# Triangular inverses turned on VectorE, a state-space stage without GpSimd, and three stages folded into their neighbours

## The reference, cut to what matters

```python
mod = silu(cond) @ w_ada + b_ada                     # shift, scale, gate, twice
h = rms_norm(x, norm1_g) * (1 + sc1) + sh1
z = h @ w_in                                         # r, k, v | wd, ad, gd (low rank) | u
y_r = rwkv7_mix(z[..., :OFF_U], state_rwkv, ...)     # 8 heads x 64, both directions
y_s = s5_mix(z[..., OFF_U:], state_ssm, ...)         # 32 groups x 16, one complex state of 64 per group
x = x + g1 * (concat(y_r, y_s) @ w_out)
h = rms_norm(x, norm2_g) * (1 + sc2) + sh2
x = x + g2 * (square(relu(h @ w_ff1)) @ w_ff2)
y = rms_norm(x, norm_f_g)
```

## Time and profile before

| what | value |
|---|---|
| median of 3 runs | 2572.7 us (2570.61 to 2576.2) |
| profiled execution, its own time | 2570.66 us |
| its span in the trace | 2568.7 us |
| front / stage u / state space | 0 to 105.2 / to 189.0 / to 472.5 us |
| GLU / low rank | to 573.3 / to 637.1 us |
| RWKV preparation / 36 steps / last step's rest and last finish | to 766.2 / to 1647.1 / to 1684.4 us |
| tail | to 2568.7 us |

### The profile page before, as it was taken

The page is one execution under the profiler, slowest core; times in us unless marked ns, Lnnn a source line. Parts: engine busy times, 40 slices in busy tenths (PEclk is TensorE's granted clock), DMA queues, the critical chain, the costliest instruction groups (busy, mean ns, idle before and its releaser), DMA issues. The chain is left out here.

```text
span 2568.7 us, 50592 instructions
## 1 busy us (share of the span) xinstructions
PE 2093.2 (81%) x21540; PEld 1373.1 (53%) x21540; DVE 1239.2 (48%) x2498; ACT 758.3 (30%) x1682; POOL 649.7 (25%) x720
## 2 busy tenths in 40 slices
PE   7673445475649899988898989769999999999998
PEld 2342334233436787677677778634555455455453
DVE  1469999730153545464546454434333333323325
ACT  2302223311123434343434444323322122112111
POOL 1407552212111212222222222113221211211253
PEclk9676777787769999999998999879999999999999
DMA  7200000441100000000000000052211011011112
GB/s 280 76 1 5 10 10 11 142 162 58 29 9 12 14 3 11 10 17 11 2 10 5 3 3 7 2 208 91 91 66 66 1 66 66 18 49 66 50 38 94
DMA packets 62691, 120.25 MB, mean 47 GB/s; under 512 B 5946, under 2 KB 25402, under 8 KB 61682
## 3 DMA queue, kind: packets, MB, share of 16 engines
q1 hardware_dynamic: 62468, 117.02, 12.9%
HBM read 97.56 MB, written 17.35 MB: 45 GB/s over the span
## 5 line engine op out<-in xcount | busy, mean ns | idle before, releaser
L83 PE MATMUL psum<-arena 128*128 128x384 bf16 (+3 forms) x2244 | 739.1, 335 | 125.1 <-ACT arena L1700 27.9
L84 PE MATMUL psum<-arena 128*128 128x384 bf16 (+3 forms) x2244 | 738.4, 335 | 0.0
L85 PE MATMUL psum<-arena 128*128 128x384 bf16 (+3 forms) x2244 | 737.6, 335 | 0.0
L1652 ACT ACTIVATE arena<-psum 128x256 f32<-128x256 f32 (+5 forms) x900 | 289.8, 333 | 529.1 <-PE psum L1524 141.4
L83 PEld LDWEIGHTS psum<-arena 128*128 128x128 bf16 (+1 forms) x2244 | 224.3, 100 | 311.5 <-issue 78.7
L85 PEld LDWEIGHTS psum<-arena 128*128 128x128 bf16 (+1 forms) x2244 | 224.9, 100 | 172.1 <-issue 9.7
L84 PEld LDWEIGHTS psum<-arena 128*128 128x128 bf16 (+1 forms) x2244 | 224.4, 100 | 164.1 <-issue 7.5
L2637 DVE TENSOR_TENSOR arena<-arena 128x384 f32<-128x384 f32 x96 | 106.9, 1113 | 234.7 <-ACT arena L2513 234.7
L1524 PE MATMUL psum<-arena 64*64 64x64 f32 x2880 | 179.7, 222 | 10.7 <-DVE arena L2201 10.7
L2652 DVE TENSOR_TENSOR arena<-arena,psum 128x512 f32<-128x512 f32 x108 | 74.2, 687 | 196.7 <-PE psum L85 196.7
L1524 PEld LDWEIGHTS psum<-arena 64*64 64x64 f32 x2880 | 159.4, 137 | 15.0 <-DVE arena L2201 14.8
(11 more groups left out here) (298 smaller groups left out, 3251.3 us busy)
## 6 DMA issues: line engine op xcount, KB each, us to landing
arena<-in_w_ff SPq DMA_DIRECT2D x16, 2048.0 KB, 8.5
arena<-in_w_ada SPq DMA_DIRECT2D x12, 2048.0 KB, 8.3
x<-arena SPq DMA_DIRECT2D x18, 512.0 KB, 2.8
arena<-x SPq DMA_DIRECT2D x18, 512.0 KB, 3.2
arena<-in_w_in SPq DMA_DIRECT2D x12, 512.0 KB, 4.0
arena<-in_x SPq DMA_DIRECT2D x9, 512.0 KB, 8.9
out_y<-arena SPq DMA_DIRECT2D x9, 512.0 KB, 2.7
arena<-in_w_out SPq DMA_DIRECT2D x2, 2048.0 KB, 10.6
```

The costliest lines, as they stand in the source:

```text
L83: nc.tensor.matmul(out, whi, xhi, start=first, stop=False)
L84: nc.tensor.matmul(out, wlo, xhi, start=False, stop=False)
L85: return nc.tensor.matmul(out, whi, xlo, start=False, stop=last)
L1652: copy = lambda out, src: nc.scalar.activation(out, src, ACT.Copy)
```

## The change

1. *Front.* Normalised blocks have nine buffers, so ACT and POOL do all nine norms ahead of the modulations; only L249 and L254 stay behind them. `w_ada` pieces 2 and 3 are queued on SP behind x blocks 0 to 5 and 0 to 7; the weights of u use the buffer of a `w_ada` piece and come last.
2. *State space.* POOL's 17-tap products go. DVE makes `gout` itself by another `complex_product` (`out_weights`), and PE makes the taps from `gout` and C. ACT loses its `gout` copies. In stage u three tap tables become two exit tables and a negated C. ys goes to memory in four parts during the GLU.
3. *Low rank.* The block goes; PE's 216 matmuls stand in the first preparation of `stage_rwkv` (`lora`, at `TO_LORA`).
4. *Inverses.* Only X is made by matmuls on levels below the last (L1523's kind), only the transpose on the last; DVE turns the copy (`flip`), and `begin` is DVE's too.
5. *Last finish* and *tail.* Two of three groups of the last finish lie among the last steps (`LAST_*` tables), and w_out and ys are loaded before the tail.

```diff
 # stage_front, SP
-            load(1)
-            load(2)
-            for b in range(TILES):
+            for b in range(NB):
                 keep_x(b)
-            weights(2)
-            weights(3)
+                if b + TILES < NB:
+                    load(b + TILES)
+                if b in (2, 4):
+                    weights(b // 2 + 1)
...
 # stage_front, ACT
-            for b in range(TILES, NB + TILES):
-                if b < NB:
-                    norm(b)
-                high(b - TILES)
+            for b in range(NB):
+                high(b)
...
 # stage_s5, ACT
                     weights(i + 1)
-                out_weights(i)
-                if more:
                     taps(i + 1)
...
 # stage_s5, PE tap
+                pe.wait_ge(ev("gout"), i + 1)
+                need(pe, ev("taps"), 2 * i)
+                        mm(ps[0:GC, TAP_FWD, g * P:g * P + GC], S.b[n][:, GB * i + g], c[:, GB * i + g], start=(n == 0), stop=(n == 1))
+                        last = mm(ps[0:GC, TAP_FWD, g * P + GC:(g + 1) * P], S.b[n][fwd, GB * i + g], flat[fwd, n, g, 0:AFTER],
...
+                        last = mm(ps[0:GC, TAP_BWD, g * AFTER:(g + 1) * AFTER], S.b[n][bwd, GB * i + g], flat[bwd, n, g, GC:],
...
 # stage_s5, DVE
+            def out_weights(i):
+                need(dve, ev("y"), 2 * (i - 1))
+                complex_product(nc.vector, dve, c, [gout[i % 2][:, 0], gout[i % 2][:, 1]], c4, p4, sc, neg_im=True, done=ev("gout"))
...
                     in_weights(i + 2)
                 if i + 1 < NBATCH:
+                    out_weights(i + 1)
                     rotor(i + 1)
                     skip(i + 1)
 # stage_rwkv, PE
+                        for n in H2:
+                            if pi < 0:
+                                yield z + TO_LORA[n]
+                                lora(n)
...
                             if l < NLEV - 1:
-                                mm(xblock(b, q, h, 0), xt, grow[b, l - 1, q, h], start=True, stop=True)
-                            last = mm(xblock(b, q, h, 1), grow[b, l - 1, q, h], xt, start=True, stop=True)
+                                last = mm(xblock(b, q, h, 0), xt, grow[b, l - 1, q, h], start=True, stop=True)
+                            else:
+                                last = mm(xblock(b, q, h, 1), grow[b, l - 1, q, h], xt, start=True, stop=True)
...
 # stage_rwkv, DVE
+            def begin(i):
+                for q in H2:
+                    dve.wait_ge(ev("xt0"), 4 * i + 2 * q + 2)
+                    nc.vector.transpose(xx[:, q, :, 0], xt0[:, q]).then_inc(ev("x0", q), 1)
+
+            def flip(i, l):
+                for q in H2:
+                    dve.wait_ge(ev("inv", l, q), i + 1)
+                    nc.vector.transpose(xx[:, q, :, 1], xx[:, q, :, 0]).then_inc(ev("flipped", l, q), 1)
+
             def merged(i, l):
+                if l > 1:
+                    flip(i, l - 1)
                 reset(i, l)
...
 # stage_rwkv, SP; stage_tail loses the same loads
+            for h in H2:
+                sp.dma_start(M.w_out[h], ins["w_out"][:, :, h * 512:(h + 1) * 512]).then_inc(ev("w_out"), 16)
+            sp.wait_ge(ev("x"), 6 * NCT)
+            for n, ys in enumerate((M.ys_hi, M.ys_lo)):
+                sp.dma_start(ys, ins["ys"][:, n]).then_inc(ev("ys"), 16)
```

More of the change, by code:

```diff
@@ L32 @@
 SEG = NC_ + 1
-TAPS = 2 * CH + 1
 GB = 4
@@ L170, in _ @@
             load(0)
+            load(1)
+            load(2)
             weights(0)
@@ L486, in s5_memory @@
     S.in_table = two(CH, G)
-    S.tap_table = [A.take(TAPS, G) for _ in range(3)]
+    S.out_table = two(CH, G)
     S.turn = two(SUP, G)
@@ L635, in stage_s5 @@
     sn = [A.take(2, GB, NC_) for _ in H2]
-    f = [A.take(2, GB, TAPS, GC) for _ in H2]
     gout = [A.take(2, GB, CH, GC) for _ in H2]
-    strip = [A.take(GB, TAPS - 2, GC, parts=GC) for _ in H2]
+    strip = [A.take(GB, 2 * CH - 1, GC, parts=GC) for _ in H2]
     toe = [A.take(GB, P) for _ in H2]
@@ L641, in stage_s5 @@
     tv = [A.take(GB * P) for _ in H2]
-    tg = [A.take(GB, TAPS, GC) for _ in H2]
     dd = A.take(G, GC, parts=GC)
@@ L1253, in stage_rwkv @@
     v = [A.take(NB, P) for _ in H2]
-    y = [A.take(NB, P), y1]
+    y = [A.take(NB, P) for _ in H2]
+    mt_at = A.at
     mt = [A.take(2, 2, 2, 64) for _ in range(6)]
@@ L1306, in periods @@
     def periods():
-        return [(pi, PERIOD * pi, pi + 1 if pi + 1 < NCT else None, pi - 1 if pi > 0 else None) for pi in range(-1, NCT + 1)]
+        return [(pi, PERIOD * pi, pi + 1 if pi + 1 < NCT else None, pi - 1 if pi > 0 else None) for pi in range(-1, NCT)]
     def entered_by(ct, d, g):
@@ L1378, in project, with lora @@
                 last.then_inc(ev("filled"), 1)
+            def lora(n):
+                pe.wait_ge(ev("lora_w_lo"), 1)
+                need(pe, ev("lora_f"), n)
+                for g in range(TG):
+                    for q in range(KD):
+                        last = split_mm(nc, ps[:, LORA.start + g, 0:GW], lw_hi[:, q, n], lw_lo[:, q, n], M.hi[:, q, cols(g)],
+                                        M.lo[:, q, cols(g)], q == 0, q == KD - 1)
+                last.then_inc(ev("lora"), 1)
             def sums(at, n):
@@ L1464, in beside @@
                         yield from entry(c, 1, 1, ENTRY[1, 1])
+                z, f = PERIOD * NCT, NCT - 1
+                for n in range(3):
+                    yield z + LAST_GATE[n]
+                    gate(z + LAST_GATE[n], f, GROUPS[n])
+                    yield z + LAST_TURN[n]
+                    turn_out(z + LAST_TURN[n], f, n, GROUPS[n])
             def score(u):
@@ L1917, in beside @@
                         split(3 * c + 2)
+                        if pi < 0:
+                            for n in range(3):
+                                yield z + TO_LORA[n]
+                                lora_low(n)
                         if c + 1 < NCT:
@@ L2713, in program @@
     keep_front = A.at
+    M.w_out = [A.t[:, M.hi_at + h * KD * 512:M.hi_at + (h + 1) * KD * 512].rearrange("p (k n) -> p k n", k=KD) for h in range(2)]
     s5_memory(M)
```

419 lines of the change are left out of this document (209 added, 210 removed).

## The result

The changed kernel takes 2531.0 us (median of 4 runs, 2529.7 to 2533.0) against 2571.7 for the kernel before; the ratio is 0.984, interval 0.983 to 0.985. That is 41 us less, where 96 had been forecast, and 1 us above the range.

The account below looks back on a forecast made before the run. Five stages had different limits, DVE in the state space, PE in the 36 steps. Terms -10 - 2.5 - 24 - 27 - 12 - 11.5 - 9 = -96 took 2570.66 to 2474.7, forecast 2475 us, range 2408 to 2530.

Parts of the forecast that it names:

- The state space: State space: first spin starts 19.5 us in, 26 earlier; seven batch intervals about even (+2.3); together -24 us.
- the taps' wait on ACT: State space: ACT's list has taps ahead of arrivals and waits for PE's tap, making a batch 31.3 us.
- Low rank and preparation: Low-rank block and first preparation: 63.8 us go, PE's 36.9 come back in the preparation; -27 us.
- The tail: Tail's start: ACT's 9.21 us wait for w_out goes, as the load moves among the last steps; -9 us.
- waits behind the flips: Steps, levels 4 and 5: PE waits about 0.7 us longer on each, 1.4 a bare step, leaving it 1.1 gain.
- the clock's term of the steps: 36 steps: PE's mean clock falls from 0.95 to 0.926, 21 us back against 33 gained, leaving -12.
- its sign of being right: Steps: a mean clock outside 0.91 to 0.96 would show the prediction wrong.
- the clock falling in the steps: Rival, steps: mean clock 0.90 costs PE 44 us more, kernel 2498; at 0.87, 73 more, 2527; chance 0.16.
- The lower bound of this term: Steps: -78 us if nothing is waited for, 89 less 11 for six steps and a little clock.
- the front: Front: w_ada queued behind 2.5 MB, 12 us at most, 9 taken, modulations start at 61; front 95 for 105.2, -10.
- 26.8 in a row: Front: POOL becomes the limit behind the modulations, 19.2 us of L249 and 7.6 of L254 without gaps.
- the last finish: Last finish: its second and third group leave the end, their 8.1 us of DVE work moving among bare steps; -11.5 us.

Follow-up runs that it names:

- run 6: The changed kernel with ScalarE's copies of the taps placed behind the arrivals and natural-order copies of a batch instead of ahead of them: 2492.8 us, ratio 0.970.
- run 3: The changed kernel without the eight flips of a step, TensorE reading X unturned, matmuls as few, the two transposes of begin kept: 2491.5 us, ratio 0.969.
- run 2: The changed kernel with the 64 merge matmuls a step put back as work nobody reads, the transposes on VectorE kept: 2560.5 us, ratio 0.996.
- Run 7: The changed kernel with the whole front stage of the kernel before (part 1 undone): 2526.8 us, ratio 0.983.
- run 1: The changed kernel with the inverses of the kernel before (part 4 undone), all else as changed: 2507.6 us, ratio 0.975.
- run 4: The changed kernel with the flips of levels 3 and 4 ahead of the two score masks on VectorE instead of behind them: 2501.3 us, ratio 0.973.
- run 9: The changed kernel with flips ahead of the score masks, ScalarE's taps behind the arrivals and the front of before: 2464.2 us, ratio 0.959.

## Why the prediction was wrong

*What held.* The state space: start (19.0 for 19.5), batch (31.8 for 31.3) and the reason, the taps' wait on ACT, which run 6 showed by moving it. Low rank and preparation -29.6 for -27. The tail -9.8 for -9. A flip 0.25 to 0.29 for 0.27. Two further agreements are luck. Step 33 came to 16.47 for 16.4, but the five steps 29 to 33 gained 0.8 together, not 1.1 each. TensorE's idle time rose by 41 us where 30 steps with 1.4 us, 42, were put in for waits behind the flips; but 26 of the 41 came with no flip at all (run 3), the flips add 15, and in step 33 the two waits rose by 0.8 only, from 0.15 and 0.28 to 0.55 and 0.67.

*What failed: the clock's term of the steps.* The step of the sum is "From a mean of 0.95 to 0.926: 797 x (0.95/0.926 - 1) = 21 back". The mean came to 0.85, outside the 0.91 to 0.96 that the prediction gave as its sign of being right, and the matmuls that remained were 69 us dearer. I had taken the fall from two rows, 1.00 in a bare step and 0.94 in a step with preparation, both with the matmuls of before; no row had TensorE as thin as the change made it. The case came out that was priced as a rival, the clock falling in the steps. The sentence of the Trainium skill beside it ("TensorE: Matmul & The Clock Gate", Part 1, the HAM clock gate), that the throttled state is the default and activity releases it, agrees with runs 3 and 2: fewer matmuls with no flips lower the clock from 0.95 to 0.89, and matmuls that nobody reads bring steps 8, 17 and 26 from 0.79, 0.80 and 0.78 to 1.00. The rule alone would not have given the size: 39 us of the loss are the flips (887 against 847), 29 of them by their place in VectorE's order. And the price per hundredth of clock was too high as I worked it: at 0.85 the prediction's formula gives 94, because it goes by the 797 us of all matmuls of before; on the 694 that are left without the 87 it gives 82, and the rows have 69. What makes up the rest was not tried. The lower bound of this term was off by itself: six steps counted at nothing are worth 15 of the 89, not 11.

*The second error, the front*, the step "so I take 9, a start at 61". The modulations start at 72.6. I priced the queue as bytes. What SP's rows show is a chain: x blocks are issued at 23.46, 28.98, 34.78, 45.75 and 51.35, each behind the store of the block whose buffer it takes, and the `w_ada` pieces stand between them; the last is issued 20 us later than before. POOL's end of 26.8 in a row came to 30.3 (76.41 to 106.68). Run 7 showed the size, 3 to 5 us; that the queue's order is the cause is read from the rows, not tried by itself.

*The third, the last finish*, -11.5 for -5.5. The end lost what was forecast: from the last step's end to the tail it takes 10.3 us instead of 21.9. But the stretch from step 35 to that end is 37.1 us at a clock of 0.65, where the kernel before took 30.9 at 0.81. DVE, with 18.9 us of work there instead of 11.5, is free enough. Of the 6.1 us, 5.1 are TensorE's busy time, 29.65 for 24.53 with 47 matmuls fewer, and 1.0 its idle time. The flips are not what costs it: with the inverses of before, run 1, the same stretch is still 5.5 us longer than before:

```profile
1586.04:1622.50 36.46, 28.76 (x438) 22.89 (x434) 17.24 (x51) 10.82 (x35) 2.33 (x8) 0.76 0.01 2
```

What is left is the groups of the finish that now lie there; no run took them out.

## What to carry to other kernels

Before work is taken off TensorE, ask whether the rest still keeps its clock: in a stretch where it waits for others anyway, most of what fewer matmuls saved was paid back by slower ones and by idle time (16 of 87 us stayed in run 3), while five bare steps, which kept a clock of 1.00 there, gained 8.4 of some 12.5. A copy or transpose that another engine adds must stand in its order ahead of the work that waits for something later; moving two calls up was worth 30 us here, and moving a copy behind what the next batch waits for 34. Price a load by its place in its queue as well as by its bytes, with every wait that stands ahead of it there; in the front, 12 us were priced at most and the load came 20 us later (read from the rows, not tried).

## What the runs showed of the hardware

The same instructions can get a different clock in two kernels. Runs 4 and 9 have the same code in the steps; the windows of step 7 in run 4 and in run 9:

```profile
910.13:930.65 20.52, 16.90 (x287) 13.58 (x286) 14.43 (x46) 9.74 (x31) 7.42 (x15) 0.92 0.02 5
```

```profile
871.32:894.67 23.35, 20.64 (x286) 17.02 (x285) 14.90 (x47) 9.89 (x31) 7.86 (x16) 0.71 0.09 25
```

2.8 us apart, at a clock of 0.92 and 0.71; step 17 has it the other way round (22.89 at 0.73 and 20.25 at 0.92). Over the 35 steps both take 857.8 us. With the flips behind the masks the sum varies too: 886.7, 879.3 and 890.2 us for the same steps in the changed kernel and in runs 6 and 7. A single step's length is therefore no measure of an edit; the sum over many is one, to some 5 us either way here, and so are steps that recur alike.
